# A two-layer hybrid backbone: the second layer's sine layers made in the opening, the last expert's output taken before the register read, and a new order of filters, combinations and rows at the change of layers

## What is computed

```python
def hyena_filters(n, w1, b1, freq, w2, b2, w3):          # from weights alone
    h = jnp.sin(freq * (feats @ w1 + b1))                # first sine layer
    h = jnp.sin(freq * (h @ w2 + b2))                    # second sine layer
    h = (h @ w3).reshape(n, HYENA_ORDER, 2, HYENA_WIDTH) # the taps
    ...                                                  # decay; two directions joined to k
    return k / jnp.sum(jnp.abs(k), axis=0, keepdims=True)

for l in range(DEPTH):                                   # DEPTH = 2
    hl = modulate(rms_norm(xl, norm_mix[l]), sh1, sc1)
    pl = hl @ w_in[l]
    xl = xl + g1 * mix_tokens(pl, ...)                   # attention, Fourier mixing, long convolutions
    h2l = modulate(rms_norm(xl, norm_ffn[l]), sh2, sc2)
    xl = xl + g2 * moe_ffn(h2l, ...)                     # 16 experts, two per token
return rms_norm(xl, norm_final)
```

## Time and profile before

| | before |
|---|---|
| median of 3 runs | 2050.45 us (2047.22 to 2055.67) |
| the profiled execution | 2048.16 us, its span 2046.5 us |
| TensorE busy | 1961.5 us (96%) |
| VectorE busy | 1715.6 us (84%) |
| ScalarE busy | 1162.8 us (57%) |
| granted clock, mean | 0.985 |
| DMA | 629.45 MB, mean 308 GB/s |
| slowest median landing in the list of DMA issues | 9.2 us |

### The profile page before, as it was taken

One profiled execution on the slowest core, in us unless ns is written; L12 is line 12 of the kernel. 1 busy time (PEld: TensorE's weight loads), 2 busy tenths in 40 slices (PEclk: granted clock), 3 DMA queues, 4 the chain that ended last, 5 costly groups with the idle time before them and its releaser, 6 DMA issues. The chain is left out here.

```text
span 2046.5 us, 25663 instructions
## 1 busy us (share of the span) xinstructions
PE 1961.5 (96%) x9322; PEld 1562.3 (76%) x9322; DVE 1715.6 (84%) x1707; ACT 1162.8 (57%) x1134; POOL 196.9 (10%) x252
## 2 busy tenths in 40 slices
PE   7999899999999999999999888899999999999997
PEld 3788558777888888888888477577888888888885
DVE  3774689898588999999999878778699999999997
ACT  2323613223257777777777345344377777777774
POOL 3000110111030000000000200000110000000001
PEclk9999999999999999999999999999999999999998
DMA  9766417666389999999999668286699999999995
GB/s 341 275 237 221 136 48 245 244 221 244 127 288 397 401 405 392 393 398 397 395 396 393 239 230 264 48 330 227 221 385 377 401 392 401 388 405 392 397 397 217
DMA packets 181457, 629.45 MB, mean 308 GB/s; under 512 B 13871, under 2 KB 16059, under 8 KB 174336
## 3 DMA queue, kind: packets, MB, share of 16 engines
q1 hardware_dynamic: 150648, 503.62, 65.3%
q0 software_dynamic: 27776, 119.98, 16.2%
q10 hardware_dynamic: 2952, 4.77, 0.7%
HBM read 597.13 MB, written 31.19 MB: 307 GB/s over the span
## 5 line engine op out<-in xcount | busy, mean ns | idle before, releaser
L1630 DVE TENSOR_TENSOR w_lo<-ring,w_hi 128x2048 fp32r<-128x2048 f32 x384 | 873.5, 2288 | 87.1 <-ACT w_hi L1493 86.6
L1493 ACT ACTIVATE w_hi<-ring 128x2048 fp32r<-128x2048 f32 x384 | 738.1, 1922 | 236.3 <-PE bank L2419 232.8
L2419 PE MATMUL bank<-w_hi,xsT_hi 128*128 128x512 f32 x1024 | 399.9, 390 | 3.3 <-DVE xsT_lo L1630 2.8
L2419 PE MATMUL bank<-w_lo,xsT_hi 128*128 128x512 f32 x1024 | 398.6, 389 | 0.0
L2419 PE MATMUL bank<-w_hi,xsT_lo 128*128 128x512 f32 x1024 | 315.5, 389 | 0.0
L1233 ACT ACTIVATE m_hi<-ring 128x1024 fp32r<-128x1024 f32 (+1 forms) x128 | 129.8, 1031 | 274.5 <-PE bank L2419 219.8
L2419 PE MATMUL bank<-m_lo,hT_hi 128*128 128x512 f32 (+1 forms) x688 | 261.7, 380 | 0.0
L2419 PE MATMUL bank<-m_hi,hT_hi 128*128 128x512 f32 (+1 forms) x640 | 247.9, 387 | 10.9 <-DVE m_lo L1630 5.1
L2419 PEld LDWEIGHTS bank<-w_hi,xsT_hi 128*128 128x128 f32 x1024 | 192.1, 188 | 46.9 <-DVE xsT_lo L1630 3.2
L2419 PE MATMUL bank<-m_hi,hT_lo 128*128 128x512 f32 (+1 forms) x592 | 223.7, 378 | 0.0
L2419 PEld LDWEIGHTS bank<-w_hi,xsT_lo 128*128 128x128 f32 x1024 | 192.2, 188 | 40.4
(11 more groups left out here) (284 smaller groups left out, 2309.7 us busy)
## 6 DMA issues: line engine op xcount, KB each, us to landing
ring<-in_w_exp_gate_dram SPq DMA_DIRECT2D x128, 1024.0 KB, 9.0
ring<-in_w_exp_up_dram SPq DMA_DIRECT2D x128, 1024.0 KB, 8.6
ring<-in_w_exp_down_dram SPq DMA_DIRECT2D x128, 1024.0 KB, 8.4
ring<-in_w_in_dram SPq DMA_DIRECT2D x44, 1024.0 KB, 6.1
work<-in_w_mod_dram POOLq DMA_DIRECT2D x40, 1024.0 KB, 5.4
ys_dram<-work POOLq DMA_DIRECT2D x32, 512.0 KB, 7.3
work<-hp_dram SPq DMA_DIRECT2D x54, 256.0 KB, 4.0
work<-mod_dram POOLq DMA_DIRECT2D x10, 1024.0 KB, 9.2
```

Of the source, the lines that this page charges most:

```text
L1493: nc.scalar.activation(w_hi[:, pos % N_SPLIT, :], raw(i), ACT.Copy).then_inc(hi_done, 1)
L1630: return nc.vector.tensor_tensor(o, a, b, op)
L2419: return nc.tensor.matmul(o, a, b, start=first, stop=last)
```

## The change

Layer 1's filter steps 0 and 1 go to the opening on all engines: step 0 behind layer 0's step 3, step 1 behind unit 5. Their weights are loaded by ScalarE's queue at the start and share layer 0's features; the kept sines (256 KB) are stored to DRAM by GpSimd, which first waits for the rest of the constants, and are loaded again beside expert 2. The last output is copied before the register read. GpSimd loads the latents' modulation rows before the last output's store, and the context's after the first gathers. In layer 1's filters the norm of filter 1 comes before the first combination. VectorE makes only combination 0 before spectrum 0 and row 0; combination 1, spectrum 1 and row 1's own root follow. TensorE makes spectrum 1 between `turn_row` 0 and block 0's projection. `spread_at`: the norm of spectrum 1 is spread first.

```diff
@@ first_chunk, plan_jobs @@
-    out = [("row", 0), ("row", 1)] if l == 0 else [("row", 0)]
+    out = [("row", 0), ("row", 1)] if l == 0 else [("row", 0), ("filter", 1)]
@@ spread_at @@
-def spread_at(l):
-    return 3 if l else 0
+def spread_at(l, o):
+    return 3 if l and o == 0 else 0
-FILTER_STEPS = 8
+AHEAD_STEPS = (2, 3, 4, 6, 5)
@@ OPENING @@
 ...
-           ("unit", 3), ("unit", 4), ("filter", 0, 4), ("unit", 5), ("filter", 0, 6), ("unit", 6), ("unit", 7),
+           ("filter", 1, 0), ("unit", 3), ("unit", 4), ("filter", 0, 4), ("unit", 5), ("filter", 1, 1), ("filter", 0, 6),
+           ("unit", 6), ("unit", 7),
 ...
@@ sync @@
                             conv_weights(l, 0)
+                            sp.wait_ge(rest_moved, HID_STORED)
@@ gpsimd @@
+            pool.wait_ge(rest_moved, CONST_MOVED)
+            pool.wait_ge(hid_ready, 2)
+            pool.dma_start(hid_dram, hid[1][:, 2:4, :]).then_inc(rest_moved, 16)
             store_spectra(0)
 ...
                     if e == 2 and l + 1 < DEPTH:
-                        for dst, src in filter_weights(l + 1):
-                            pool.dma_start(dst, src).then_inc(filt_loaded[l + 1], 16)
+                        pool.wait_ge(rest_moved, HID_STORED)
+                        pool.dma_start(hid_out[1], hid_dram).then_inc(rest_moved, 16)
 ...
+                    if e == NE + 1:
+                        pool.wait_ge(w_used, ready_at(NE - 1, 7) + l * PER_LAYER)
+                        pool.dma_start(B_bc[:, 0, :], mod_dram[l + 1, 0, 0, :].partition_broadcast(P)).then_inc(ab_loaded, 16)
+                        pool.dma_start(A_bc[:, 0, :], mod_dram[l + 1, 0, 1, :].partition_broadcast(P)).then_inc(ab_loaded, 16)
 ...
-                    pool.dma_start(B_bc, rows_of(l + 1, 0)).then_inc(ab_loaded, 16)
-                    pool.dma_start(A_bc, rows_of(l + 1, 1)).then_inc(ab_loaded, 16)
+                    pool.dma_start(B_bc[:, 1, :], mod_dram[l + 1, 1, 0, :].partition_broadcast(P)).then_inc(ab_second, 16)
+                    pool.dma_start(A_bc[:, 1, :], mod_dram[l + 1, 1, 1, :].partition_broadcast(P)).then_inc(ab_second, 16)
@@ scalar @@
+            for dst, src in filter_weights(1):
+                act.dma_start(dst, src).then_inc(filt_loaded[1], 16)
 ...
-                    for _ in split_high(("in", l + 1, "v")):
-                        pass
+                    ahead = split_high(("in", l + 1, "v"))
                     for g in (2, 3):
+                        for _ in range(2):
+                            next(ahead)
                         filter_step(l + 1, g)
-                    weigh(l, early_blocks(l), GOT_EARLY[l])
+                    weigh(l, [T[0]], GOT_EARLY[l])
                     filter_step(l + 1, 5)
-                    squares(2 * (l + 1), range(2), lambda k: act.wait_ge(combined, T_BEFORE[l] + k + 1))
-                    root(2 * (l + 1), 0, 2)
-                    filter_step(l + 1, 7)
+                    for k in range(2):
+                        act.wait_ge(combined, T_BEFORE[l] + k + 1)
+                        square_of(2 * (l + 1), k, k, hrow[:, 1, :])
+                        if k == 0:
+                            root(2 * (l + 1), 0, 1, 0)
+                            weigh(l, [T[1]], GOT_EARLY[l])
+                            filter_step(l + 1, 7)
@@ vector @@
                     if l and tb:
                         low_rows(l, tb - 1)
+                        filter_step(l, 7)
+                        inverse_rms(ph, tb, 1, tb)
 ...
-                if l + 1 < DEPTH:
-                    filter_step(l + 1, 0)
-                    filter_step(l + 1, 1)
+                take_ys(NE - 1, 1)
                 o = over[l]
                 dve.wait_ge(dve_took, TAKEN[("tot", l)])
                 busiest = dve.value_load(most[0:1, 0:1], min_val=0, max_val=512)
-                take_ys(NE - 1, 1)
 ...
-                    made = taps(l + 1, 0)
-                    for _ in low:
-                        next(made)
-                    for _ in made:
-                        pass
-                    filter_step(l + 1, 3)
+                    for g in (2, 3):
+                        filter_step(l + 1, g)
+                        for _ in range(2):
+                            next(low)
                     filter_step(l + 1, 4)
-                    for k in range(2):
-                        combine(l, k, T[k])
+                    filter_step(l + 1, 6)
+                    combine(l, 0, T[0])
                     filter_step(l + 1, 5)
-                    filter_step(l + 1, 6)
-                    inverse_rms(2 * (l + 1), 0, 2)
+                    inverse_rms(2 * (l + 1), 0, 1, 0)
                     dve.wait_ge(ab_loaded, 32 * (2 * (l + 1) + 1))
                     modulated(hrow[:, 0, :], 0, 0)
-                    filter_step(l + 1, 7)
+                    combine(l, 1, T[1])
@@ tensor @@
                     if kind == "row":
                         turn_row(0, tb, tb, hrow[:, tb % 2, :])
+                    elif kind == "filter":
+                        tap_spectra(l, 1)
 ...
-                    elif l + 1 < DEPTH:
-                        filter_step(l + 1, 0)
                     down(e - 1, 1 - par, 1)
 ...
-                if l + 1 < DEPTH:
-                    filter_step(l + 1, 1)
 ...
-                    for g in range(2, FILTER_STEPS):
+                    for g in AHEAD_STEPS:
                         filter_step(l + 1, g)
```

More of the change, by code:

```diff
@@ L132, in plan_jobs @@
     for step in first_chunk(l):
-        if step[0] == "row":
+        if step[0] == "filter":
+            out.extend((n, filter_taker(n)) for n in filter_jobs(l, 7))
+        elif step[0] == "row":
             for half in range(2):
@@ L303, in hybrid_kernel @@
     for l in range(DEPTH):
-        for g in range(FILTER_STEPS if l else 0):
+        for g in AHEAD_STEPS if l else ():
             jobs += [(n, filter_taker(n)) for n in filter_jobs(l, g)]
@@ L408, in hybrid_kernel @@
         out_tmp = lent(7680, 512)
-        hid = [a.rearrange("p (i n) -> p i n", i=4) for a in (lent(11264, 1024), mixed[:, 2560:3584])]
+        hid = [a.rearrange("p (i n) -> p i n", i=4) for a in (lent(11264, 1024), mixed[:, 3328:4352])]
+        hid_out = [hid[0][:, 2:4, :], work[:, 7616:8128].rearrange("p (i n) -> p i n", i=2)]
         pq = lent(11264, 1024).rearrange("p (i n) -> p i n", i=2)
@@ L412, in hybrid_kernel @@
         decay = [t.rearrange("p (i n) -> p i n", i=2) for t in (mixed[:, 1024:2048], work[:, 6144:7168])]
-        feats = [mixed[0:33, 2304:2560], work[0:33, 7168:7424]]
-        w1 = [mixed[0:33, 2048:2112], work[0:33, 7424:7488]]
-        w2 = [mixed[0:64, 2112:2240], work[0:64, 7488:7616]]
+        feats = mixed[0:33, 2304:2560]
+        w1 = [mixed[0:33, 2048:2112], mixed[0:33, 4352:4416]]
+        w2 = [mixed[0:64, 2112:2240], mixed[0:64, 4416:4544]]
         norm_at = [[filt_abs[l][o][0][:, 0, :].rearrange("p (j n) -> p j n", j=4) for o in range(2)] for l in range(DEPTH)]
@@ L462, in hybrid_kernel @@
         ys = work[:, 2048:4096].rearrange("p (i n) -> p i n", i=2)
-        over_xT = work[:, 0:1024].rearrange("p (k n) -> p k n", k=KB)
+        over_xT = hT_flat[:, 1024:2048].rearrange("p (k n) -> p k n", k=KB)
         over_hT = hT_flat[:, 0:1024].rearrange("p (k n) -> p k n", k=KB)
@@ L523, in hybrid_kernel @@
         const_rows, four_rows = (nc.inline_tensor(a, name=n).ap() for n, a in mirrored_constants().items())
+        hid_dram = nc.dram_tensor("hid_dram", (P, 2, SEQ), F32, kind="Internal").ap()
         spec_dram = nc.dram_tensor("spec_dram", (DEPTH, P, 2 * 4 * HY), F32, kind="Internal").ap()
@@ L537, in hybrid_kernel @@
         const_loaded = sem("const_loaded")
-        const_rest = sem("const_rest")
+        CONST_MOVED, HID_STORED, HID_LOADED = 16, 32, 48
+        rest_moved = sem("rest_moved")
         small_loaded = sem("small_loaded")
@@ L642, in hybrid_kernel @@
         SQUARES = [0, 4, 8, 12, 14]
-        ROOTS = [0, 1, 5, 7, 9]
+        ROOTS = [0, 1, 5, 8, 10]
         ROWS_AT = {(0, 0): 0, (0, 1): 4, (1, 0): 8, (1, 1): 12}
@@ L733, in filter_weights @@
         def filter_weights(l):
[L734 to L735 removed]
+            return ((w1[l], A["filt_w1"][l]), (w2[l][:, 0:64], A["filt_w2"][l]), (w2[l][:, 64:128], A["filt_w2"][l]))
         def tap_weights(l):
@@ L774, in conv_rows @@
                     i += 1
+            sp.dma_start(feats, A["k_feats"]).then_inc(filt_loaded[0], 16)
             for dst, src in filter_weights(0):
@@ L1298, in _ @@
                     rows_high(tb)
+                    if l and tb == 0:
+                        root(2 * l, 1, 1, 1)
                 if late_rows(l):
@@ L1337, in _ @@
                         late_square(late_rows(l)[1])
-                        root(2 * l, 2, 2, 1)
+                        root(2 * l, 2, 2, 2)
                     if c == 2:
@@ L1818, in late_norm @@
             def late_norm(l, low):
-                inverse_rms(2 * l, 2, 2, 1)
```

(14 more changed lines are left out.)

14 lines of the change are left out of this document (3 added, 11 removed).

## The result

The changed kernel takes 2061.45 us (median of 4 runs, 2058.12 to 2064.61) against 2050.99 of the kernel before: ratio 1.0046, 95% interval 1.0031 to 1.0062. Timed once more among the experiments it had 1.0044 (1.0030 to 1.0058). So by the ratios it is slower by 9 to 9.4 us; I had forecast 2.5 to 3, in a range that ended at 2059. The profiled execution took 2058.12, span 2056.6, 10.1 more than before's.

The account below looks back on a forecast made before the run. TensorE was taken to bound the experts, leaving gain or loss to the opening (+1.4) and the change of layers (+2.2 or +0.8). Taking 3 us gave 2051.2 for the profiled run and 2053 us as forecast, range 2045 to 2059.

Parts of the forecast that it names:

- rest nought: Everything outside the opening and the change of layers: the forecast's sum counted no change in time there.
- Copy first: Change of layers: taps start at 1134.3 in place of 1140.03, 5.7 us won, after 1.9 us waiting, at high clock.
- The clock at the first spectrum: Layer 1, between last tap and first spectrum: TensorE's clock falls, costing 2.45 us.
- the mark: Start of block 1 in layer 1's first projection, whose shift passes to the end; forecast +2.2 us.
- Spectrum 1 between the row and block 0: Layer 1: TensorE waits 5.9 us, clock low again, spectrum uncovered and eats the gain; block 0 starts 2.2 us later.
- Rival 2: Change of layers: the full 5.7 us pass through if the spectrum behind the row is covered; 2044.8 us, chance 0.10.
- The opening: Start of the kernel: added sine products and their wait delay units 6, 7 and the first row by 1.4 us.
- rival 5: Opening: each sine brings table loads of 1.28 us, +2.6 us, 2055.5 us; chance 0.02.
- 1: Rival, layer 1's spectra: clock stays high at the first or both, mark -0.3 or -2.3, about 2050.5 us; chance 0.25.
- 3: Rival, layer 1's spectra: the low clock does not come back, mark +14.7, 2066.5 us with the opening; chance 0.06.
- 4: Rival, opening: TensorE's wait for the sine becomes the whole chain of both layers, +5 us, 2057 us; chance 0.02.

Follow-up runs that it names:

- e1: Kernel before, with each bank up to the end of layer 0's routing taken two places further on; 2053.25 us, ratio 1.0011.
- e5: Kernel before, with only the last expert's output copied earlier, between layer 1's two sine layers on VectorE; 2050.01 us, ratio 0.9994.
- e7: Kernel of e5 plus nine unused filling products on TensorE ahead of layer 1's taps; 2049.84 us, ratio 0.9991.
- e8: Kernel before, with GpSimd waiting for the constants and storing 256 KB to a spare place ahead of layer 0's spectra; 2053.11 us, ratio 1.0007.
- e11: The changed kernel measured again, with no further edit; 2060.25 us, ratio 1.0044.
- e2: Changed kernel, with the bank rotation set back by two up to the end of layer 0's routing; 2055.58 us, ratio 1.0033.
- e12: Kernel of e2 measured again, with no further edit; 2058.6 us, ratio 1.0034.
- e4: Kernel of e2 plus unused filling products, 6 ahead of layer 1's second norm and 12 ahead of row 0; 2052.85 us, ratio 1.0005.
- e9: Kernel of e2 plus 6 unused filling products ahead of layer 1's second norm only; 2060.49 us, ratio 1.0046.
- e13: Kernel of e9 measured again, beside e12; 2055.95 us, ratio 1.0018.
- e3: Kernel of e2 with the order of before from layer 1's first norm on, keeping opening sines and early copy; 2049.55 us, ratio 0.9993.
- e6: Kernel of e3 with GpSimd's sine store behind both spectrum stores and no wait for the constants; 2050.8 us, ratio 0.9990.

## Why the prediction was wrong, point by point

*What moved, against what was forecast.* The table sets the distances between fixed points of the profiles beside the terms of the forecast, in us. Where a stretch scatters, it gives means: of the five profiles with the opening of before (before, e1, e5, e7, e8) and of the ten with the new one.

| stretch | forecast | measured | from |
|---|---|---|---|
| start to layer 0's first block | +1.4 | +1.4 | means 64.4 and 65.8 |
| to the last routing product | 0 | 0 | means 507.2 and 507.1 |
| to the first expert product | 0 | +4.2 | 12.12 before, 16.29 now; 16.36 in e11, 14.98 in e1 |
| first to last expert product | -0.45 | -0.3 | 551.98 and 551.64 |
| last expert product to block 1 | +2.65 | +4.1 | 50.15 and 54.24 |
| block 1 to the end | 0 | +0.5 | means 864.1 and 864.6 |

The 0.45 is the sine product that leaves the experts; with the 2.2 of the forecast it makes 2.65 on this scale. The forecast column adds up to 3.6, the measured one to 9.9, against the 9 to 9.4 of the ratios. The ratios of e1 and e2 would give the third row only 2.3 to 2.7 us and leave about 3 for the first two; the profiles place no such loss there. By either account the largest part of what I lacked is the bank.

*The step that failed: "rest nought".* I had said that what the change can win or lose lies in two places, the opening and the change of layers. It lost 4.2 us in a third, between layer 0's routing and its experts, while the experts themselves kept their length. I asked for each added product when its operands are ready and who waits for it, but not which bank it takes and whose bank that changes, 500 us later. The change of `OPENING` is in the diff and the modulo is in `begin`; no row of before shows it, since there nobody waits. Without this term the time stays inside my range: e2 and e12 have 2055.58 and 2058.6.

*Copy first.* Right: 2.00 us of wait (1.9 forecast), the taps at the high clock (7.10 for 9.47 us in the earlier trace rows). It was not certain: of ten profiles with this wait nine have the taps high, e4 has not.

*The clock at the first spectrum.* The mechanism was right, its start was one product too late. I let it fall behind the second norm product and counted 1.85 us for that. The clock is 0.88 from 1154 to 1155 and 0.50 behind: it fell as the norm started, behind 3.13 us of waiting, and the norm took 3.38. That is the 1.5 us by which the mark was mis-sized (4.1 against 2.65), and it lies ahead of the row: the row is turned 33.6 us behind the last product, where my numbers give 32.3. e9 and e13 win it back with spectrum 0's share. Spectrum 0 lost 1.9 us (7.29 in place of 5.40 for its first 12 records), 2.45 were counted.

*Spectrum 1 between the row and block 0.* Right in mechanism and size: wait 5.99 (5.9), clock 0.50 until 1178, block 0 directly behind the filling products, 2.75 us from the end of block 0 to block 1. The Trainium skill (TensorE: Matmul & The Clock Gate, HAM oscillation) describes short groups with waits between them that all start low; the trace agrees for the groups behind the waits of 3.13 and 5.99 us (clock 0.50 from 1155 and from 1172), not for the taps behind 2.00, which ran at 1.00.

*What I had not asked.* Whether the order could be had better without this part. With the order of before almost the whole gain of the early taps arrives: they start 5.1 us sooner behind the last product, and block 1 comes 4.7 us sooner (45.45 against 50.15). With the new order and the norm filled (e9) the row itself does come early, 30.3 us behind the last product and not 33.1, but the spectrum behind it takes more than that back. Rival 2 named this condition, that the spectrum is covered, and my objection to it was right for the changed kernel.

*The opening.* One pair of profiles shows +3.0 at layer 0's first block, but little of it can be laid on the added products. 1.5 arise in the row at 18.99, ahead of every added product: 6.64 us for 8 records in place of 5.13. The low clock ahead of the spectra was then shorter (0.50 from 38.6 to 42, before from 35.5 to 42.3), the spectra took 15.72 in place of 16.79, and at their end (58.02 for 56.72) the offset is 1.3. The other 1.7 arise as the first rows are turned, behind 2.80 us of waiting and at half the clock: 1.94 in place of 1.07 us for 8 records. Over the five profiles with the opening of before the block starts at 63.3 to 66.3, mean 64.4; over the ten with the new one at 64.4 to 66.9, mean 65.8. So it is +1.4, as forecast, but with such spreads the match to a tenth is luck. The second sine product runs at 36.49; 34.85 was forecast, and the taps before it are 1.6 late. At the weights' split near 165 the means are 164.2 and 166.8, 1.2 us more than at the block, where I had counted nothing; at the last routing product they are 571.6 and 572.9, and this 1.2 is gone. e3's ratio would leave 3.3 us spent before the change of layers (4.7 won there, 1.4 at the end), but its interval is 2 us to either side and holds 1.4 as well. Whether the new opening costs 1.4 or 3 us is not settled.

*Tables.* No table load stands beside the two sines at 36.02 and 40.23: rival 5 is out. The Trainium skill (ScalarE: Activation LUTs, What ACT_TABLE_LOAD costs) charges a change of table set; here there was none to charge. The 2.66 us that the Trainium skill gives there for a change isn't seen elsewhere in this kernel either: in the trace of before a load of 1.28 us starts at 517.00, directly behind the instruction in front of it, and the next one starts at 518.29.

*The rivals.* None of the five came true. 1 and 3 went by the clock, which fell twice and came back twice; 2 fell, since the spectrum had no cover; 4 because the wait for the sine was short. The sixth, the bank, was missing. The range was too narrow above: 2059 held only mis-sized steps, not a mechanism that I had overlooked. That the change would lose and not win was forecast for the right reason, spectrum 1 behind the row; of the measured loss this reason and the opening make up a little over half.

## What to carry to other kernels

Where buffers are dealt out by a running number, an added product changes the buffer of every later one: compute the assignment of both versions up to the next fixed point, and look at who is taken late there. When work is moved behind the row that everything waits for, ask not only what is late before it but what covered it where it stood; here spectrum 1 was free beside VectorE's second combination. Moving it cost 8.8 us with the two falls of the clock, and still some 4.6 with both waits filled (50.09 in e4 against 45.45). And one pair of profiles can't place a loss of 2 us: compare distances between two near points, over several kernels that share the stretch. No version beat the kernel before measurably; e3, e6 and e7 are at 0.9990 to 0.9993 with 1 inside the interval. The early copy in the old order wins 2.3 us at the change of layers in e5 and 2.2 in e7, and I would keep it, though their times don't show it clear of noise. The sines would need a place that costs neither the opening nor the end, which was not tried.

## What the runs showed of the hardware

The granted clock differs between executions of the same instructions. The 26 filling records ahead of the last routing product take 5.65 us in twelve profiles and some 8 us in three (e1, e4, e5), and layer 0's eight tap records at 19 us, behind the same products in all, take 5.12 to 6.64. The eight tap records of layer 1 behind a wait of 2.0 us take 7.10 or 7.11 us in nine profiles and 8.80 in e4. The runs of one kernel spread by 4 to 14 us (before: 2047 to 2060), while the distance from the last expert product to block 1 repeats within 0.7 us (50.15, 49.80 and 50.08 with before's code, 54.83 and 54.20 in e2 and e12).
